# A mixture of experts in 32-slot tiles of plain fp32 on TensorE's four column positions

## The reference, cut to what matters

```python
aff = jax.nn.sigmoid((t @ router_w).astype(jnp.float32))
score = aff + router_bias.astype(jnp.float32)
group_score = lax.top_k(score.reshape(-1, N_EXPERT_GROUPS, per_group), 2)[0].sum(-1)
_, gsel = lax.top_k(group_score, TOPK_GROUPS)
_, esel = lax.top_k(jnp.where(emask, score, NEG_INF), TOPK_EXPERTS)
...
for e in range(N_EXPERTS):
    he = jax.nn.silu(t @ w_gate[e]) * (t @ w_up[e])
    y = y + combine[:, e:e + 1] * (he @ w_down[e])
```

## Time and profile before

| what | value |
|---|---|
| median of 3 runs | 2703.89 us (2699.5 to 2704.99) |
| the profiled execution's own time | 2704.23 us |
| its span | 2702.4 us |
| granted TensorE clock, mean | 0.985 of full speed |
| TensorE matmul busy | 2608.3 us, 97% |
| VectorE busy | 1866.2 us, 69% |
| ScalarE busy | 1316.0 us, 49% |
| read from HBM | 632.79 MB, 237 GB/s over the span |

### The profile page before, as it was taken

The page is one execution under the profiler, slowest core; times in us unless marked ns, Lnnn a source line. Parts: engine busy times, 40 slices in busy tenths (PEclk is TensorE's granted clock), DMA queues, the critical chain, the costliest instruction groups (busy, mean ns, idle before and its releaser), DMA issues.

```text
span 2702.4 us, 33550 instructions
## 1 busy us (share of the span) xinstructions
PE 2608.3 (97%) x13165; PEld 2171.7 (80%) x13165; DVE 1866.2 (69%) x2436; ACT 1316.0 (49%) x1687; POOL 108.4 (4%) x110
## 2 busy tenths in 40 slices
PE   5799999999999999999999999999999999999998
PEld 2499998877888888887788688888878888888886
DVE  7978867866778899998877665756554554555445
ACT  2445545544445677876543244444544434443443
POOL 1000000000000000000223300000000000000000
PEclk9899989999999999999999999999999999999999
DMA  9997875527778899999454354554555555655553
GB/s 376 380 369 291 307 250 208 206 72 252 270 265 287 341 370 378 379 376 343 164 186 171 140 195 156 187 186 171 187 189 194 191 190 187 194 192 189 189 195 115
DMA packets 159418, 641.18 MB, mean 237 GB/s; under 512 B 11115, under 2 KB 11196, under 8 KB 116520
## 3 DMA queue, kind: packets, MB, share of 16 engines
q1 hardware_dynamic: 151416, 593.61, 60.9%
q0 software_dynamic: 5264, 27.21, 2.8%
q10 hardware_dynamic: 2592, 18.35, 1.8%
HBM read 632.79 MB, written 6.34 MB: 237 GB/s over the span
## 4 chain that ended last, share of the span: by engine, by line
PE 84%; DVE 7%; DMA 5%; ACT 2%; issue 1%; SPq 0%; ACTq 0%; DVEq 0%
PE ps L2219 82%; DMA raw<-in_stream 2%; DVE w_lo L1324 2%; DMA under_r<-in_stream 1%; ACT w_hi L780 1%; DMA under_w_lo<-in_stream 1%; DVE raw L1400 1%; DMA arena<-in_stream 1%; DVE under_w_lo L1400 1%; DVE under_w_hi L1400 0%; PE ps L2381 0%; PE ps L2884 0%; DVE under_r L1418 0%; PE ps L2636 0%; DVE arena L2126 0%
## 5 line engine op out<-in xcount | busy, mean ns | idle before, releaser
L1324 DVE TENSOR_TENSOR w_lo<-raw,w_hi 128x1024 fp32r<-128x1024 f32 x888 | 1087.1, 1232 | 628.6 <-ACT w_hi L780 621.9
L780 ACT ACTIVATE w_hi<-raw 128x1024 fp32r<-128x1024 f32 x888 | 936.4, 1059 | 1035.2 <-PE ps L2219 1010.6
L2219 PE MATMUL ps<-w_hi,r_two 128*128 128x512 f32 x3072 | 967.4, 393 | 11.6 <-DVE w_lo L1324 5.0
L2219 PEld LDWEIGHTS ps<-w_hi,r_two 128*128 128x128 f32 x3072 | 578.9, 188 | 135.4 <-DVE w_lo L1324 9.1
L2219 PE MATMUL ps<-w_lo,r_two 128*128 128x512 f32 x1536 | 599.8, 390 | 0.0
L2219 PE MATMUL ps<-h_two,w_hi 128*128 128x256 f32 (+1 forms) x2048 | 554.7, 344 | 4.0 <-DVE w_lo L1324 4.0
L2219 PE MATMUL ps<-w_hi,h_two 128*128 128x512 f32 x1728 | 541.5, 391 | 6.3 <-DVE w_lo L1324 3.6
L2219 PE MATMUL ps<-h_two,w_lo 128*128 128x256 f32 x1536 | 432.5, 282 | 0.0
L2219 PEld LDWEIGHTS ps<-h_two,w_hi 128*128 128x128 f32 x2048 | 355.4, 192 | 50.2 <-issue 5.2
L2219 PEld LDWEIGHTS ps<-w_hi,h_two 128*128 128x128 f32 x1728 | 324.4, 188 | 77.0 <-issue 4.4
L2219 PEld LDWEIGHTS ps<-w_lo,r_two 128*128 128x128 f32 x1536 | 289.4, 188 | 59.1 <-issue 0.5
(11 more groups left out here) (352 smaller groups left out, 1585.8 us busy)
## 6 DMA issues: line engine op xcount, KB each, us to landing
raw<-in_stream SPq DMA_DIRECT2D x460, 1024.0 KB, 5.4
arena<-in_stream SPq DMA_DIRECT2D x40, 1024.0 KB, 7.4
under_r<-in_stream SPq DMA_DIRECT2D x58, 512.0 KB, 6.2
arena<-in_mod_units ACTq DMA_DIRECT2D x16, 1024.0 KB, 5.7
arena<-in_stream SPq DMA_DIRECT2D x25, 512.0 KB, 6.8
under_w_hi<-in_stream SPq DMA_DIRECT2D x8, 1024.0 KB, 17.5
under_w_lo<-in_stream SPq DMA_DIRECT2D x8, 1024.0 KB, 16.7
under_h<-in_stream SPq DMA_DIRECT2D x13, 512.0 KB, 5.9
```

What stands on the lines that cost most here:

```text
L780: act.activation(dst, src, ACT.Copy).then_inc(hi_ready, 1)
L1324: dve.tensor_tensor(low, src, high, ALU.subtract).then_inc(lo_ready, 1)
L2219: return pe.matmul(o, a, b, start=start, stop=stop)
```

## The change

- Tokens are sorted into 12 tiles of 32 slots (`SLOTS_ALL` = 384). The four groups are ranked by size and have 4, 2, 1 and 1 tiles of their own; four "loose" tiles take what does not fit, whatever group it is of.
- A stage (48 in all, `STAGES`) takes the same unit of the same expert number of all four groups: four transfers of whole units, into `raw` at even stages and into `under_w` (the place of `w_hi` and `w_lo`) at odd ones. Nothing is split any more.
- Each stage has three rounds on TensorE (`expert_round`). A round has four tiles, each on its own 32 columns of the array: the stationary operand is 128 x 32 tokens, the result goes to partitions 32c to 32c+31. Operands are plain fp32. Gate and up: 16 x 4 products of 128 columns a round; down: 4 x 4 of 512. Round 0 is the largest group's four tiles, round 1 the other own tiles, round 2 the loose ones.
- For round 2 ACT and DVE copy the unit of each loose tile's group, chosen at run time, into a fixed place (`loose`).
- The hidden values of 384 slots are turned with three transposes and copied by ACT; `down` reads them. Sums lie in `acc` as three times 128 slots; `unsort` has 6 products instead of 4, one group of them ahead of the last stage and three behind it.
- The ring of six slots goes, and so does `landing_of`'s case for it. The next phase's weights are fetched after stage 46 and split after the last round (`hi`) and after the last `add_unsorted` (`lo`).
- The router ranks the groups and works out the loose tiles' groups: about 15 more small DVE steps ahead of the sort, and nine behind it.

```diff
+SLOT = 32
+BASE_TILES = (4, 2, 1, 1)
+TILES = 12
+SLOTS_ALL = TILES * SLOT
+ROUNDS = TILES // 4
+PER = 4
+
+
+def stage_table():
+
+    pairs = lambda j, first, last: [(kind, j, i) for i in range(first, last) for kind in ("gate", "up")]
+    table = pairs(0, 0, 4)
+    for j in range(PER):
+        table += pairs(j + 1, 0, 1) if j + 1 < PER else []
+        table += [("down", j, i) for i in range(4)]
+        table += pairs(j + 1, 1, 4) if j + 1 < PER else []
+    return table
+
+
+STAGES = stage_table()
+LAST_UP = STAGES.index(("up", PER - 1, 3))
+MOE_GROUPS = len(STAGES) * ROUNDS // 8
+MOE_SKIPS = 12 * N_EXP - 4 * MOE_GROUPS
+ROW_STAGES = tuple(STAGES.index(("down", 2, 0)) + 1 + q for q in range(4))
...
+        acc = under_r.rearrange("p a n -> p (a n)")[:, 0:ROUNDS * D].rearrange("p (r n) -> p r n", r=ROUNDS)
+        sorted_t = under_h.rearrange("p a n -> p (a n)")[:, 0:DC * SLOTS_ALL].rearrange("p (c n) -> p c n", c=DC)
+        loose = (at(0, UNIT), at(UNIT, UNIT), under_r[:, 1, D:2 * D], under_h[:, 1, D:2 * D])
+        landing = [t.rearrange("p s n -> p (s n)") for t in (raw, under_w)]
+        perm_t = at(10240, ROUNDS, T)
+        hidden_t = at(11520, 5, SLOTS_ALL)
+        moe_act, moe_hid = at(13440, SLOTS_ALL), at(13824, SLOTS_ALL)
...
+            def expert_unit(st, r):
+
+                kind, j, i = STAGES[st]
+                unit = 12 * j + {"gate": 2 * i, "up": 2 * i + 1, "down": 8 + i}[kind]
+                src = sp_units[bass.ds(48 * group[r] + (ADA_UNITS + BASE["moe"] + unit), 1)].rearrange("a p n -> (a p) n")
+                sp.dma_start((raw, under_w)[st % 2][:, r, :], src).then_inc(sem(f"under_landed{st % 2 + (2 if r else 0)}"), 16)
+
+            for st in range(len(STAGES)):
+                if st == 1:
+                    sp.wait_ge(half_done, 8 * gm)
+                if st >= 2:
+                    sp.wait_ge(half_done, 8 * gm + ROUNDS * (st - 2) + 1)
+                    sp.wait_ge(hi_ready, 8 * gm + ROUNDS * (st - 1))
+                    sp.wait_ge(lo_ready, 8 * gm + ROUNDS * (st - 1))
+                for r in range(4):
+                    if st == 0:
+                        sp.wait_ge(lo_ready, 8 * gm - 6 + 2 * r)
+                    if st >= 2 and r == 1:
+                        sp.wait_ge(half_done, 8 * gm + ROUNDS * (st - 2) + 2)
+                    expert_unit(st, r)
+            last_even = len(STAGES) - 2
+            sp.wait_ge(half_done, 8 * gm + ROUNDS * last_even + 2)
+            sp.wait_ge(hi_ready, 8 * gm + ROUNDS * (last_even + 1))
+            sp.wait_ge(lo_ready, 8 * gm + ROUNDS * (last_even + 1))
             stream(group_base("hyena"), group_base("ffn_in0"))
...
+            loose_rank = [act.value_load(route[0:1, 4 + c:5 + c], min_val=0, max_val=3) for c in range(2)]
+
+            def loose_weights(st):
+
+                act.wait_ge(sem(f"under_landed{st % 2}"), 16 * (FIRST_LANDINGS + st // 2 + 1))
+                act.wait_ge(sem(f"under_landed{st % 2 + 2}"), 16 * FIRST_LANDINGS + 48 * (st // 2 + 1))
+                if st:
+                    act.wait_ge(half_done, 8 * gm + ROUNDS * st)
+                for c, half in ((0, 0), (0, 1), (1, 0)):
+                    src = landing[st % 2][:, bass.ds(UNIT * loose_rank[c] + HALF * half, HALF)]
+                    copy(loose[c][:, half * HALF:half * HALF + HALF], src).then_inc(hi_ready, 1)
+
+            def expert_act(p):
+
+                if p:
+                    act.wait_ge(sem("hidden_pair"), p)
+                act.activation(moe_act, ps[:, 2 * (p % 2), 0:SLOTS_ALL], ACT.Silu).then_inc(sem("hidden_silu"), 1)
+
+            def expert_turned(p):
+
+                act.wait_ge(sem("hidden_t"), p + 1)
+                copy(hidden_t[:, p % 5, :], ps[:, 7, 0:SLOTS_ALL]).then_inc(sem("hidden_hi"), 1)
...
+            for st in range(len(STAGES)):
+                loose_weights(st)
+                kind, j, i = STAGES[st - 1]
+                if st and kind == "gate":
+                    expert_act(4 * j + i)
+                if st and kind == "up":
+                    expert_turned(4 * j + i)
+                if st % 2 and st // 2 < LATE_UNITS:
+                    load_mod(late_slot, st // 2 + ADA_UNITS)
...
+            act.wait_ge(half_done, 8 * group_base("hyena"))
+            for k in range(3):
+                hi(group_base("hyena"), k)
...
+                for c, first in ((1, HALF), (2, 0), (3, 0)):
+                    src = landing[st % 2][:, bass.ds(UNIT * loose_rank[c] + first, UNIT - first)]
+                    dve.tensor_copy(loose[c][:, first:UNIT], src).then_inc(lo_ready, 1)
...
+            def expert_hidden(st, p):
+
+                dve.wait_ge(half_done, 8 * gm + ROUNDS * st)
+                dve.wait_ge(sem("hidden_silu"), p + 1)
+                if p:
+                    dve.wait_ge(sem("hidden_t"), p)
+                for r in range(ROUNDS):
+                    o = slice(r * P, (r + 1) * P)
+                    ins = dve.scalar_tensor_tensor(moe_hid[:, o], moe_act[:, o], comb_slot[:, r, p // 4:p // 4 + 1],
+                                                   ps[:, 2 * (p % 2) + 1, o], ALU.mult, ALU.mult)
+                ins.then_inc(sem("hidden_pair"), 1)
...
+                for r in range(ROUNDS):
+                    dve.wait_ge(half_done, 8 * gm + ROUNDS * st + r + 1)
+                    o, new = acc[:, r, cut], ps[:, 4 + r, :]
+                    if j:
+                        dve.wait_ge(sem("down_out"), ROUNDS * (4 * (j - 1) + cb) + r + 1)
+                    ins = dve.tensor_tensor(o, o, new, ALU.add) if j else dve.tensor_copy(o, new)
+                    if j == PER - 1:
+                        ch(ins)
+                        ins = dve.tensor_tensor(o, o, row[:, cut], ALU.mult)
+                    ins.then_inc(sem("down_out"), 1)
...
+            for st in range(len(STAGES)):
+                kind, j, i = STAGES[st - 1]
+                if st and kind == "up":
+                    expert_hidden(st, 4 * j + i)
+                loose_weights(st)
+                if st == 1:
+                    place_weights()
+                if st % 2 == 0 and 0 < st <= 2 * LATE_UNITS:
+                    if st == 2:
+                        dve.wait_ge(sem("c_ready"), 2)
+                    late_modulation(st // 2 - 1)
+                if st + 1 in ROW_STAGES:
+                    gate_diag(ROW_STAGES.index(st + 1))
+                kind, j, i = STAGES[st]
+                if kind == "down":
+                    down_out(st, j, i)
+            for cb in range(4):
+                add_unsorted(cb)
+            for k in range(3):
+                lo(group_base("hyena"), k)
...
+            def expert_round(st, r, ready=None):
+
+                kind, j, i = STAGES[st]
+                for n in range(4 if kind == "down" else DC):
+                    if ready:
+                        ready(n)
+                    for c in range(4):
+                        tile, place = slice((4 * r + c) * SLOT, (4 * r + c + 1) * SLOT), slice(c * SLOT, (c + 1) * SLOT)
+                        w_rows = loose[c] if r == 2 else (raw, under_w)[st % 2][:, (0, (1, 1, 2, 3)[c])[r], :]
+                        if kind == "down":
+                            ins = mm(ps[place, 4 + r, :], hidden_t[:, (4 * j + n) % 5, tile], w_rows[:, 512 * n:512 * n + 512], n == 0, n == 3)
+                        else:
+                            bank = 2 * (i % 2) + (kind == "up")
+                            ins = mm(ps[place, bank, r * P:(r + 1) * P], sorted_t[:, n, tile], w_rows[:, P * n:P * n + P],
+                                     n == 0, n == DC - 1)
+                ins.then_inc(half_done, 1)
...
+            def unsort(cb):
+
+                pe.wait_ge(sem("down_out"), ROUNDS * (16 if cb >= 2 else 13 + cb))
+                for h in range(TH):
+                    for r in range(ROUNDS):
+                        ins = mm(ps[:, 2 * cb + h, :], perm_t[:, r, h * P:(h + 1) * P], acc[:, r, cb * 512:cb * 512 + 512],
+                                 r == 0, r == ROUNDS - 1)
+                    ins.then_inc(sem("unsorted"), 1)
...
+            for st, (kind, j, i) in enumerate(STAGES):
+                before_this = STAGES[st - 1]
+                if kind == "gate" and 4 * j + i >= 2:
+                    pe.wait_ge(sem("hidden_silu"), 4 * j + i - 1)
+                if kind == "up" and 4 * j + i >= 2:
+                    pe.wait_ge(sem("hidden_pair"), 4 * j + i - 1)
+                if st == LAST_UP + 1:
+                    turn_hidden(4 * PER - 1)
+                if kind == "down" and i == 0:
+                    pe.wait_ge(sem("hidden_hi"), 4 * j + 4)
+                    pe.wait_ge(sem("perm_t_ready"), 2)
+                pe.wait_ge(sem(f"under_landed{st % 2}"), 16 * (FIRST_LANDINGS + st // 2 + 1))
+                for r in range(ROUNDS):
+                    if r == 1:
+                        pe.wait_ge(sem(f"under_landed{st % 2 + 2}"), 16 * FIRST_LANDINGS + 48 * (st // 2 + 1))
+                    if r == 2:
```

(44 more changed lines are left out.)

485 lines of the change are left out of this document (109 added, 376 removed).

## The result

The changed kernel takes 2718.4 us (median of 4 runs, 2713.8 to 2721.1), the kernel before 2702.3 us beside it. The ratio is 1.0058, 95% interval 1.0039 to 1.0077: slower by 0.6%, some 16 us. The profiled execution has a span of 2719.3 us.

The account below looks back on a forecast made before the run. It took TensorE and DMA as nearly equal limits. DMA's sum, 595 + 586 + 3.4 + 3.4 + 15.5 = 1203, exceeded TensorE's 1180; plus 2 and 8 gave 1213 against 1298.8, so 2618 us, range 2595 to 3075.

Parts of the forecast that it names:

- the queue can hand out an instruction every 30 ns or less: TensorE's queue in the expert stages: read off two 24-column loads starting within 0.03 us, supporting 30 ns per gate/up pair.
- The clock is taken at 2.4 GHz: TensorE in the expert stretch: full clock assumed, as the granted share was 1.00 in nearly the whole stretch before.
- Four at once, and the pairs' prices: TensorE products on four column positions overlap: 30 ns per gate/up pair, 107 per down pair, 369 + 165 = 534 us.
- 534 + 18 us for the stages: TensorE's stages: 534 us of pairs, 15 of transposes, row products and one unsort group, 3 for turning the places.
- The ends: Around the stages: TensorE starts stage 0 at about 612 us; three unsort groups take 15.5 us after; 2 us more behind.
- two at once: Rival, chance 0.21: program order blocks the queue, so a product costs one pass of 109 ns; stages 1000 us, kernel 3053.
- one at a time: Rival, chance 0.08: plain fp32 on column positions does not overlap; 2000 us in place of 534, kernel near 4050 us.
- A dearer pair: Rival, chance 0.16: gate/up pairs cost more than 30 ns; break-even at 40 ns, while 55 ns gives 2893 us.
- The DMA term: Transfers of the expert stages: 220 MB at 376 GB/s take 586 us, a stage of four units 11.2 us.
- the own range of the forecast case: Whole kernel: 2595 to 2665 us around 2618, chance 0.55, for the likeliest case alone.
- no loss: Expert stages: 8 us were added for stages where the two limits take turns; the range's lower end assumed none of it.
- So the DMA stream does not break: Transfers for two stages ahead: copies end some 4 us after landing, while the stage between still has 7 us to transfer.

Follow-up runs that it names:

- e4: The change with only 32 of 2048 columns per weight transfer after stage 1, so nearly no weight traffic: 2581.9 us, ratio 0.9559.
- e7: On e2, round 1 as two products of 64 stationary columns, the fourth tile taking the third group's weights: 2593.1 us, ratio 0.9598.
- e3: The change with gate and up products reading 160 weight columns instead of 128, same instructions: 2720.8 us, ratio 1.0068.
- e1: The change with round 0's four tiles, which share weights, as one product of 128 stationary columns: 2648.4 us, ratio 0.9799.
- e6: The change with gate and up recut so one product reads 128 columns of each, in 4 KB pieces: 2612.9 us, ratio 0.9675.
- e9: As e4, with gate and up products reading 64 weight columns instead of 128, same instructions: 2575.0 us, ratio 0.9534.
- e2: On e1, round 1's two tiles of the second group as one 64-column product beside two of 32: 2886.8 us, ratio 1.0684.

## Why the prediction was wrong

**The step that failed** is the one sentence on supply: "That also shows that the queue can hand out an instruction every 30 ns or less." It rested on two loads of 24 columns 0.03 us apart. For a few instructions, and even for 256, that holds. It says nothing about where the next 256 come from. Before, the stretch of 372 us had some 3350 instructions, so 256 lasted 28 us; the change uses them up in 3.7. The term that was missing from the sum is these gaps: 113 us of issue. The Trainium skill (Vector Engine (DVE) Microarchitecture Reference, Instruction fetch and dispatch (NX sequencer)) says that an instruction is exactly 64 bytes, for VectorE; 16.4 KB for each burst of 256 agrees with that for TensorE. With that width, the growth of instructions could have been turned into bytes per microsecond before the run.

**The second error hangs on the first.** "The clock is taken at 2.4 GHz": between 612 and 1295.7 us the granted share was 0.96,

```profile
612.00:1295.70 683.70, 567.27 (x13930) 423.61 (x13920) 235.73 (x321) 161.62 (x183) 1.29 (x2) 0.96 0.83 322
```

and TensorE busy 567.3 us with work that takes 528.6 in e4, at a share of 1.00. So the account closes: from e4's 1154.5 to 1295.7 are 141 us, 103 of them more issue (113.2 - 10.1) and 39 more busy time. Of these, some 27 us are the lower clock (a share of 0.96 over 683.7 us, an estimate). The other 12 or so are largely the recorded tail of the last matmul before each of 43 more gaps, some 0.2 us each: 128 pairs are recorded with 3.70 us and take 3.5 from start to start. The clock falls behind pauses: from 651 to 653 us, behind six gaps, the granted share is 0.50, and 114 pairs take 5.10 us. In e7, which hardly pauses, it is 1.00 from 612 to 1100 us, but in e3, with 43 pauses, 0.99; that the pauses bring it down was not tested apart.

**What was right.**
- *Four at once, and the pairs' prices.* 128 pairs in 3.70 us are 29 ns each, the tail of the last included; 64 down pairs in 7.07 us are 110 ns (forecast 30 and 107). The forecast 534 + 18 us for the stages stand against 542.5 in e4, with 10 of issue in it.
- *The ends.* Stage 0 at 611.95 (forecast 612), the three unsort groups behind the last stage 15.72 us (15.5), and 4 us more behind the stretch (2).
- *The rivals "two at once" and "one at a time"* fell with the first burst. The rule of the Trainium skill that the prediction cited for the former (TensorE: Matmul & The Clock Gate, The mechanism), matmuls that start and end in program order, does not make the outcome that it was read to make. Nor do the four column tiles fall short of four, as the prediction's estimate of 630 us had it, from the Trainium skill's speedup of 2.38 for three (TensorE: Matmul & The Clock Gate, Measured speedup vs the span model): in e4, the products of four tiles at once fit, with the 18 us of the rest, into 542 us, where one after the other would take 2000 by the prediction's sum.
- *"A dearer pair"* came nearest, for a reason that it did not name. TensorE's 683.7 us less 165 for down and 18 for the rest are 40.7 ns per gate or up pair, and its break-even was 40. The time is about the same as before because the starved rate happens to lie there.

**What was off in size.** The DMA term, 586 us at 376 GB/s, is too high for pieces of 8 KB on a queue that never runs dry: at e7's 416 GB/s the 220 MB take 530. So without starvation the two limits are nearer to each other than I had them, and e7 came out at 2593, 2 us below the own range of the forecast case. The ends of that range also don't follow from what is named for them: DMA at 379 GB/s and no loss gives 2606, not 2595, and a pair at 35 ns with three times the loss gives 2672, not 2665. "So the DMA stream does not break" was right in its reasons and wrong in its premise: slots come free when TensorE is done with them, and with TensorE 113 us late the share fell to 0.83.

The time lies inside the range of 2595 to 3075 and the sign is wrong: 0.36 stood on slower, all of it for reasons of the array, none for the supply of code.

## What to carry to other kernels

When a change cuts a product into small ones, count instructions per microsecond as one counts bytes. Here 256 of them, one packet of 16 KB, came every 3.5 us at best on idle queues and every 5.2 to 6.5 us beside weights at full rate. Gate and up stages with 14 ns of work an instruction (the change) or 18 (e1, e3; estimated from their rounds of 3.4 to 4.6 us) left TensorE waiting for code; with 23 ns (e7) 5 us of waiting were left, with 29 (e6) none. The cure is more columns per instruction, not fewer microseconds of work: products that share a stationary operand can share a pass, and tiles that share weights a wider one, but only with neighbours of their own width. A gap whose releaser the profile calls issue, after a round number of instructions, is the sign to look for, with the queue of instructions beside it.

## What the runs showed of the hardware

- TensorE's instructions come in packets of 16.4 KB that travel beside the weights on the DMA engines. Without weight traffic one came every 3.5 us (e9), beside it mostly every 6.2 us and more (bursts of 3.70 + 2.47, and of 4.55 + 1.65 in e3). At half the traffic 76 of 113 us of issue remain. The packet takes about 1 us either way and the work goes on 2.2 to 2.6 us after its start; the traffic delays that start, and what exactly it waits behind is open.
- Bursts without a gap go with pauses of the weights. In the change 508 pairs run without one from 649.7 to 666.3 us: the DMA share there is 0.22 until 655.3 and 0.67 until 661 us, and packets start at 650.8, 655.2 and 659.2 us, 3.4 to 4.4 apart.
- Of three mixes of column positions, those of equal width ran at once, 4 x 32 (e4) and 2 x 64 (e7). 64 + 32 + 32 (e2) did not: 0.705 us for a step of 0.21. Other mixes were not tried.
- A quarter more columns in each gate and up product cost no time clear of the noise (2720.8 against 2718.4 us, with the clock at 0.99 instead of 0.96), and halving them on idle queues saved none (2575.0 against 2581.9).
- With the DMA engines busy throughout (share 1.01), stages whose gate and up weights come in pieces of 4 KB moved 393 GB/s, those in pieces of 8 KB 416.
